# Down projection: half-width correction products in ten of eleven blocks, a merged first sum, and the scaling of e moved to the gate projection

## The reference, cut to what matters

```python
gu = _rmsnorm(h, g_ffn) @ w_gate_up                                  # FFN
h = h + (jax.nn.silu(gu[..., :D_FF]) * gu[..., D_FF:]) @ w_down      # down projection, D_FF = 5632
e = _rmsnorm(p_l @ w_ple, g_ple)
h = h + jax.nn.sigmoid(h @ w_ple_gate) * e                           # gate projection
return h                                                             # then a final _rmsnorm
```

## Time and profile before

| | |
|---|---|
| median of 3 runs | 1173.64 us (1172.48 to 1173.68) |
| span of the profiled execution | 1170.3 us |
| PE busy | 1159.2 us, 99% |
| DVE busy | 999.4 us, 85% |
| ACT busy | 562.8 us, 48% |
| chain that ended last | PE 94%, DVE 3%, DMA 1%, ACT 1%, issue 1% |
| granted clock of PE | 9 tenths or more of full speed (2.4 GHz) in all 40 slices |
| loads | 200 GB/s over the span, 65% of the DMA engines' time in the down stage |

### The profile page before, as it was taken

The page is one execution under the profiler, slowest core; times in us unless marked ns, Lnnn a source line. Parts: engine busy times, 40 slices in busy tenths (PEclk is TensorE's granted clock), DMA queues, the critical chain, the costliest instruction groups (busy, mean ns, idle before and its releaser), DMA issues.

```text
span 1170.3 us, 30909 instructions
## 1 busy us (share of the span) xinstructions
PE 1159.2 (99%) x12429; PEld 1039.3 (89%) x12429; DVE 999.4 (85%) x1563; ACT 562.8 (48%) x808; POOL 55.3 (5%) x80
## 2 busy tenths in 40 slices
PE   8999999999999999999999999999999999999997
PEld 7888988888888899899998999989989999999886
DVE  6788599678867898898989989888899999998687
ACT  6545654555545744443444444444444444444443
POOL 2122310100000200000000000000000000000000
PEclk9999999999999999999999999999999999999999
DMA  7767766766566566666666666666666666667561
GB/s 252 231 207 207 236 193 203 236 180 198 172 223 195 173 218 196 197 195 214 206 198 195 194 211 211 197 196 193 208 198 211 205 199 203 209 200 232 171 192 75
DMA packets 193386, 234.93 MB, mean 201 GB/s; under 512 B 8011, under 2 KB 153778, under 8 KB 193041
## 3 DMA queue, kind: packets, MB, share of 16 engines
q1 hardware_dynamic: 187984, 221.08, 60.2%
q0 software_dynamic: 3968, 11.89, 3.5%
q10 hardware_dynamic: 1360, 0.92, 0.3%
HBM read 226.89 MB, written 7.43 MB: 200 GB/s over the span
## 4 chain that ended last, share of the span: by engine, by line
PE 94%; DVE 3%; DMA 1%; ACT 1%; issue 1%; SPq 0%; DVEq 0%; ACTq 0%
PE acc L2293 13%; PE acc L1895 11%; PE acc L1897 11%; PE acc L1899 11%; PE acc L2334 7%; PE acc L2296 6%; PE acc L2295 6%; PE acc L2274 6%; PE acc L2276 5%; PE wrk L2274 4%; PE wrk L2276 4%; PE acc L2337 2%; PE acc L2336 2%; DMA raw<-in_w_in_dram 1%; DVE hl L970 1%; PE wrk L2052 1%
## 5 line engine op out<-in xcount | busy, mean ns | idle before, releaser
L970 DVE SCALAR_TENSOR_TENSOR hl<-raw,hl 128x1024 f16<-128x1024 f32 x414 | 492.9, 1218 | 58.7 <-ACT hl L606 56.0
L606 ACT ACTIVATE hl<-raw 128x1024 f16<-128x1024 f32 x414 | 420.5, 1052 | 172.3 <-DMA raw<-in_w_down_dram 90.4
L2293 PE MATMUL acc<-nrm,hl 128*128 128x264 f16 x1344 | 274.8, 276 | 0.0
L1897 PE MATMUL acc<-nrm,hl 128*128 128x264 f16 x920 | 253.9, 276 | 0.0
L1899 PE MATMUL acc<-nrm,hl 128*128 128x264 f16 x920 | 253.9, 276 | 0.0
L1895 PE MATMUL acc<-nrm,hl 128*128 128x264 f16 x920 | 253.9, 276 | 0.0
L2295 PE MATMUL acc<-nrm,hl 128*128 128x264 f16 x672 | 185.5, 276 | 0.0
L2296 PE MATMUL acc<-nrm,hl 128*128 128x264 f16 x672 | 185.5, 276 | 0.0
L2293 PEld LDWEIGHTS acc<-nrm,hl 128*128 128x128 f16 x1344 | 128.9, 98 | 17.8 <-DVE tg L1452 0.2
L2334 PE MATMUL acc<-big,hl 128*128 128x264 f16 x704 | 130.2, 276 | 0.0
L1895 PEld LDWEIGHTS acc<-nrm,hl 128*128 128x128 f16 x920 | 90.2, 98 | 13.1 <-issue 0.3
(11 more groups left out here) (493 smaller groups left out, 2226.3 us busy)
## 6 DMA issues: line engine op xcount, KB each, us to landing
raw<-in_w_gate_up_dram SPq DMA_DIRECT2D x168, 512.0 KB, 4.6
raw<-in_w_down_dram SPq DMA_DIRECT2D x88, 512.0 KB, 4.1
raw<-in_w_in_dram SPq DMA_DIRECT2D x80, 512.0 KB, 4.7
raw<-in_w_out_dram SPq DMA_DIRECT2D x32, 512.0 KB, 4.7
raw<-in_w_ple_gate_dram SPq DMA_DIRECT2D x32, 512.0 KB, 5.2
state<-in_state_hgrn_dram POOLq DMA_DIRECT2D x8, 512.0 KB, 7.2
out_new_hgrn_sample_dram<-state POOLq DMA_DIRECT2D x8, 512.0 KB, 5.2
raw<-in_w_gate_up_dram SPq DMA_DIRECT2D x16, 256.0 KB, 3.2
```

The lines of the kernel that those rows point to most:

```text
L606: nc.scalar.activation(hi[:, st.hl_slot(j, half), :], raw[:, st.raw_slot(j), :], ACT.Copy, scale=WSCALE).then_inc(hi_done, 1)
L970: stt(lo[:, st.hl_slot(j, half), :], raw[:, st.raw_slot(j), :], WSCALE, hi[:, st.hl_slot(j, half), :], ALU.mult, ALU.subtract).then_inc(lo ...
L1897: mm(out, wh, x_lo[:, kt, :], start=False, stop=False)
L2293: mm(out, wh, n_hi[:, kt, :], start=jj == 0 and kk == 0, stop=False, skip_group_check=bool(up))
```

## The change

The blocks of the down stage that use half-width corrections become 0 to 9, five pairs instead of four; only block 10 stays plain. The token sums cover 20 K-tile pairs instead of 16, in ten pieces instead of seven; new buffers and shared tiles (`s16_all`, `sf_all`, `pt_all`, `mixed`) hold them and what had lain there, and DVE waits once for the store out of `s_final`. In `hl` the high and low part of a slot now lie side by side, so that the sums of a pair read one regular pattern, and the first two sums are one operation of 2 x 8 x 128 elements, in which w12 is read twice through a step of 0. In DVE's down group the sums of pair 0 are made at the end of the group before, and the others move by one place. `scale_e` moves from the down groups into the gate groups, behind the fourth and fifth split of each, and in the last group behind split 5; `rstd_bc` moves to a tile of its own, and ACT no longer waits for `e_ready`.

```diff
-DOWN_PAIRS = (2, 4, 6, 8)
-DOWN_T = ((0, 8), (8, 10), (10, 12), (12, 13), (13, 14), (14, 15), (15, 16))
-T_SOON, T_LATE = (1, 3), (0, 2, 4, 5, 6)
+DOWN_PAIRS = (0, 2, 4, 6, 8)
+DOWN_T = ((0, 8), (8, 10), (10, 12), (12, 14), (14, 15), (15, 16), (16, 17), (17, 18), (18, 19), (19, 20))
+T_SOON, T_LATE = (1, 3, 6, 7, 8), (0, 2, 4, 5, 9)
...
-        hl = sb("hl", [P, 2, HL_SLOTS * BLOCK_KT * COLS], F16)
-        hi, lo = (hl[:, n, :].rearrange("p (s c) -> p s c", s=HL_SLOTS) for n in range(2))
+        hl = sb("hl", [P, HL_SLOTS, 2, BLOCK_KT * COLS], F16)
+        hi, lo = (hl[:, :, n, :] for n in range(2))
...
-            act.wait_ge(e_ready, KT)
...
             def weight_sums(s, s0, f, done, n):
 
-                w = hl[:, :, s0 * BLOCK_KT * COLS:(s0 + 2) * BLOCK_KT * COLS]\
-                    .rearrange("p h (q k m c) -> p h q k m c", k=2, m=2, c=P)
+                w = hl[:, s0:s0 + 2].rearrange("p s h c -> p (s h c)").rearrange("p (n k m c) -> p n k m c", k=2, m=2, c=P)
                 if f == 0:
-                    for k, x in enumerate((w[:, :, :, 1, 1], w[:, :, :, 0, 0])):
-                        last = tt(s[:, k], w[:, :, :, 0, 1], x, ALU.subtract)
-                    last.then_inc(done, 1)
+                    x, y = w[:, :, 0, 0], w[:, :, 0, 1].unsqueeze(1).to_broadcast([P, 2, 8, P])
+                    x = bass.AP(x.tensor, x.offset, [list(x.ap[0]), [3 * P, 2]] + [list(d) for d in x.ap[1:]])
+                    tt(s[:, 0:2], y, x, ALU.subtract).then_inc(done, 1)
                     return
                 dve.wait_ge(done, n + f)
-                x = w[:, :, :, 0, 0] if f == 1 else w[:, :, :, 1, 0]
-                tt(s[:, f + 1], x, s[:, 0 if f == 1 else 2], ALU.subtract).then_inc(done, 1)
+                tt(s[:, f + 1], w[:, :, f - 1, 0], s[:, f], ALU.subtract).then_inc(done, 1)
...
-                    dve.wait_ge(used, S_DOWN.block(i, j - 3 - (S_DOWN.bpg - 8 if u < 2 else 0)) + 1)
-                weight_sums(s_sum[u % 2], S_DOWN.hl_slot(j, half), f, down_sums, (i - 1) * DOWN_SUMS + 3 * u)
+                    dve.wait_ge(used, S_DOWN.block(i, j - 3 - (S_DOWN.bpg - 2 * len(DOWN_PAIRS) if u < 2 else 0)) + 1)
+                weight_sums(s_sum[(u + half) % 2], S_DOWN.hl_slot(j, half), f, down_sums, (i - 1) * DOWN_SUMS + 3 * u)
...
+            dve.wait_ge(sf_out, 16 * QUADS)
...
-                scale_e(0)
+                for f in range(3):
+                    down_sum(1, 1, 0, f)
                 for j in range(2, AHEAD):
                     split(S_DOWN, 1, j, 1)
...
-                sums(0)
                 split(S_DOWN, i, 4, half)
+                sums(1)
                 if evac:
                     evac()
                 else:
                     down_evac(i - 1, 1 - half)
                 split(S_DOWN, i, 5, half)
-                sums(1)
-                for j in range(6, 9):
-                    split(S_DOWN, i, j, half)
-                sums(2, (0,))
+                sums(2)
+                split(S_DOWN, i, 6, half)
+                split(S_DOWN, i, 7, half)
+                sums(3)
+                split(S_DOWN, i, 8, half)
                 next_low(i - 1)
                 split(S_DOWN, i, 9, half)
-                sums(2, (1, 2))
+                sums(4)
                 split(S_DOWN, i, 10, half)
-                sums(3)
                 ahead(0)
-                scale_e(i)
-                for j in range(1, AHEAD):
+                ahead(1)
+                if not nxt:
+                    for f in range(3):
+                        down_sum(i + 1, 1 - half, 0, f)
+                for j in range(2, AHEAD):
...
             def evac_gate(i):
+                dve.wait_ge(e_ready, i * TPG + TPG)
                 for n in range(TPG):
                     gate_tile(i, n)
...
-            group(S_GATE, 0, lambda: (dve.wait_ge(e_ready, KT), evac_gate(0)),
-                  between=lambda n: next_low(S_DOWN.groups - 1) if n == 1 else None)
+            def behind_split(i, n):
+
+                if n in (3, 4):
+                    scale_e(i * 2 + n - 3)
+
+            group(S_GATE, 0, lambda: evac_gate(0),
+                  between=lambda n: next_low(S_DOWN.groups - 1) if n == 1 else behind_split(0, n))
             with dve.Fori(1, S_GATE.groups - 1) as i:
-                group(S_GATE, i, lambda: evac_gate(i), between=lambda n: gained(i - 1) if n == 5 else None)
+                group(S_GATE, i, lambda: evac_gate(i), between=lambda n: gained(i - 1) if n == 5 else behind_split(i, n))
             last_gate = S_GATE.groups - 1
...
             split(S_GATE, last_gate, 5)
+            scale_e(2 * last_gate)
+            scale_e(2 * last_gate + 1)
             y_taken(0)
+            dve.wait_ge(e_ready, KT)
             gate_tile(last_gate, 0)
...
-                    u = j // 2 - DOWN_PAIRS[0] // 2
+                    u = (j - DOWN_PAIRS[0]) // 2
                     q = 2 * (j - DOWN_PAIRS[0])
-                    last = corrections(b, slot, s_sum[u % 2], 2 * (j % 2), ff_hi, ff_lo, 4 * j,
+                    last = corrections(b, slot, s_sum[(u + half) % 2], 2 * ((j - DOWN_PAIRS[0]) % 2), ff_hi, ff_lo, 4 * j,
```

More of the change, by code:

```diff
@@ L343, in build @@
         ps8 = sb("ps8", [P, 8])
-        lbt = sb("lbt", [P, 4, 8])
-        nomlb = sb("nomlb", [P, 8])
+        mixed = sb("mixed", [P, TOK])
+        at = [0, 64, 128, 192, 208, 224, 256, 264]
+        o_smp, o_sq, o_ms, ss_o, rs_o, lbt, nomlb = (mixed[:, a:b] for a, b in zip(at, at[1:]))
+        o_smp, o_sq, o_ms = (x.rearrange("p (h b) -> p h b", b=NSAMP) for x in (o_smp, o_sq, o_ms))
+        ss_o, rs_o = (x.rearrange("p (h a) -> p h a", a=2) for x in (ss_o, rs_o))
+        lbt = lbt.rearrange("p (n k) -> p n k", k=8)
         ss = sb("ss", [P, 3])
@@ L348, in build @@
         rt = sb("rt", [P, HEADS * 2])
[L349 to L355, removed]
+        pt_all = sb("pt_all", [P, 4 * TOK], F16)
+        pt_hi, pt_lo = (pt_all[:, 2 * n * TOK:2 * (n + 1) * TOK].rearrange("p (k t) -> p k t", t=TOK) for n in range(2))
+        dt16 = [x.bitcast(F16) for x in (mix[:, :], big[:, 2 * FFW:2 * FFW + 4 * TOK], spare[:, 660:660 + 4 * TOK])]
+        dt16 += [s16_all[:]]
+        dt16 += [x.rearrange("p a t -> p (a t)").bitcast(F16) for x in (a32[:], tg32[:], gate_t[:, 2:4])]
+        dt16 += [sf_all[:].bitcast(F16), pt_all[:], gate_t[:, 0:2].rearrange("p a t -> p (a t)").bitcast(F16)]
+        dt16 = [x.rearrange("p (h f q t) -> p h f q t", h=2, f=4, t=HALF_T) for x in dt16]
         h_sq, h_ssq = a32[:, 0, :], a32[:, 1, :]
         k_pack = a32[:].rearrange("p a t -> p (a t)")[:, 0:4 * P].rearrange("p (h t) -> p h t", h=4)
-        rstd_bc, smp_sums = gate_t[:, TPG - 1, :], gate_t[:, 0, 0:P]
+        rstd_bc, smp_sums = mixed[:], gate_t[:, 0, 0:P]
         diag, diag_smp = tg32[:, 0, 0:SEQ], tg32[0:NSAMP, 1, 0:NSAMP]
@@ L817, in _ @@
                     act.wait_ge(mean_ready, 2)
[L818 removed]
+                    nc.scalar.activation(rs_o, rs_o, ACT.Sqrt).then_inc(rstd_ready, 1)
                 if b == SAMPLE_ROOT_AT:
                     act.wait_ge(mean_ready, 3)
[L821 removed]
+                    nc.scalar.activation(o_sq, o_sq, ACT.Sqrt).then_inc(rstd_ready, 1)
                 if b in O_MIX_AT:
@@ L2172, in sample_sums @@
                 pe.wait_ge(osq_ready, 1)
-                mm(out[:, 0:64], ones[:], o_sq[:].rearrange("p h b -> p (h b)"), start=True, stop=True).then_inc(job_done, 1)
+                mm(out[:, 0:64], ones[:], o_sq.rearrange("p h b -> p (h b)"), start=True, stop=True).then_inc(job_done, 1)
                 yield
```

42 lines of the change are left out of this document (20 added, 22 removed).

## The result

The changed kernel takes **1194.97 us** (median of 4, 1193.43 to 1195.73) against 1173.06 us of the kernel before on the same chip: ratio 1.0189, 95% interval 1.0177 to 1.0201, that is 21.9 us more where 10.4 were forecast. The spans of the two profiled executions, 1170.3 and 1193.9 us, are 23.6 us apart; that is what is accounted for here. In each execution of the changed kernel 1.8 to 1.9 us lie around the span. So the 3.3 us that stood ahead of the prediction between span and median are not all around the program: the profiled execution of the kernel before (1170.3 + 1.8) is as quick as the shortest of its four, that of the changed kernel is the longest of its four, and so the spans lie further apart than the medians.

A forecast was written before the change was run, and what follows sets the result against it. PE bounds the whole kernel, but DVE becomes the down stage's bound at 29.6 us a group: 9.7 us there plus 1.0 at the tail, +10.7 on 1173.64, about 1184 us; range 1175 to 1195.

The forecast's parts named there:

- PE's gain: Down stage: ten of eleven blocks fast instead of eight, 2.66 us in all; PE alone falls to 27.80 us a group.
- the fused sum: Down pairs: the first two sums become one operation of 2048 elements, 1.25 us, 0.06 less a pair.
- VectorE's work: Down group: 29.25 us of DVE work against 27.80 us of PE, so DVE becomes the bound of the stage.
- The load waits: Down groups: DVE's waits for loads, taken as 0.35 us a group, between no wait and today's 1.07 us.
- late loads: Down stage: loads landing after 4 us and more instead of 3.5 add about 1 us over six groups.
- The bounds: Down group: 28.95 us with no wait, 30.7 with the extra 0.3 us and waits grown by half; 29.6 taken.
- The first group: First fast down group: DVE late through more early token sums; about 28.4 us, +0.2.
- The gate stage's start: Start of the gate stage: ACT loses its wait for e, worth nothing as PE runs there.
- The tail: Last gate group: two more scalings, 1.24 us less 0.23, put the kernel's end back by 1.0 us.
- a starting lead: Range: with load waits, the reason for 4 us on each side, as one execution can't size them.
- A rival's condition: Down stage, DVE stays hidden: needs a group of at most 27.8 us or 8.5 us lead; 1172.0 us; chance 0.13.

The follow-up runs named there:

- the run with four pairs: Changed kernel with the fifth pair alone taken back and the sums in their old places; layout, fused sum and moved scaling stay: 1172.91 us, ratio 1.0007.
- the two together: Changed kernel without the fifth pair and with the last gate group's e scaled earlier: 1172.04 us, ratio 0.9997 to the kernel before.
- the run with GpSimd: Changed kernel with the low halves of h and the scalings of e moved to GpSimd in the down groups: 1201.81 us, ratio 1.0251.

## Why the prediction was right and wrong

*PE's gain, the fused sum, VectorE's work: right.* Fast blocks come 2.51 us apart where PE does not wait, the fused sum takes 1.224 us for 1.25, VectorE's own work is 29.26 us a group for 29.25. That this last agrees to 0.01 us is luck: five fused sums at 0.026 us less make 0.13 us, so other terms were as much too small. Which engine takes over and where PE feels it came as said: PE waits at the sums, 34 times by up to 0.5 us at the dependent ones (L1533).

*The load waits: the step that failed.* The prediction set 0.35 us a group, "since DVE itself is now late", and 1 us in all for late loads: 3.1 us over the stage. The run with half-size loads shows 10.9 us over the stage, 1.59 us in a steady group. The 7.8 us between the two are what the down stage took beyond the forecast (7.7). Being late gives nothing here: SP's waits are on VectorE's own splits, so when VectorE is late the loads are issued as much later. How long a split waits is set by VectorE's work between the split that frees a slot and the one that needs it, and by how many loads fly together.

The prediction counted that work (5.1 us in place of 5.7) for block 2 alone, which split 10 releases and which waited before; in the new order block 2 waits for nothing. It passed over block 1, which split 9 releases. Before, 6.8 us lay between the end of split 9,

```profile
944.39 1.22 DVE L970 SCALAR_TENSOR_TENSOR hl<-raw,hl 128x1024 f16<-128x1024 f32 x1
```

and the split of block 1 (952.39 in the earlier trace rows). In the new order VectorE is there at 961.99, 5.0 us after split 9 (957.02), while the load (4.4), ACT (1.1) and the hand-overs between them take 5.8. And block 4, the fifth split, was to wait no longer; it waits 0.53 us, not for the copy of p1 but for its load, the third of a burst.

The bounds held the measured group: the terms of the upper one, 28.95 + 0.3 + 1.5 x 1.07, make 30.86 us (the 30.7 there is a slip), and 30.85 were measured. The value taken between the bounds was the wrong one.

*The first group:* 1.0 us over its old length, where 0.2 were set. With half-size loads it takes 28.23 us, and 28.4 were forecast: the rest is load waits again.

*The gate stage's start: a step that was missing.* The prediction looked at the gate stage for the moved scaling only, and called ACT's lost wait "worth nothing as PE runs there". It did not ask what stands ahead of `last_evac` in VectorE's and ACT's lists once VectorE is the bound. Of the 11.0 us by which the median passed the forecast, 5.2 us are there.

*The tail: right, a little too large.* 1.0 us was forecast; 0.7 us came, by the run with four pairs, by the run with the scalings earlier, and by the two together. The prediction had PE stand for DVE there before the change already; the profile of the kernel before lists no such wait, and that of the changed kernel lists 0.84 us.

In sum, against a forecast of 10.7 us on the span: 7.7 more in the down stage, 5.2 at the gate stage's start, 0.2 ahead of the stage, 0.3 less at the tail, 23.5 of the 23.6 us seen. The median of the changed kernel lies 11.0 us above the forecast and 0.03 us inside the range. That it lies inside is luck: the range was set for load waits and a starting lead, and 5.2 us come from the gate stage's start, which it did not have.

*A rival's condition:* for DVE to stay hidden, the lead asked for was 6 x 1.4 us. Against PE's own 27.80 us a group it is 6 x 1.8 = 10.8 us; with the 3.6 us read there, the rival was still less likely.

## What to carry to other kernels

When an edit turns an engine into the bound, do not take its waits as gone because it is late. If the loads that it waits for are released by its own progress, the waits come along. Look at each load by itself, in the new order of the list: the time from its release to its landing, with the loads that fly beside it, less the work that the engine has in between. Then go to the end of the stage and ask what the late engine still has ahead of the work that lets the next stage begin. And weigh the prize first: here 0.38 us a group of TensorE was bought with 2.7 us of sums on an engine that had 1.07 us to spare.

## What the runs showed of the hardware

A load of 512 KB landed 3.5 us after its issue when alone, 4.4 us when another had been issued 1.75 us ahead, 6.2 us as the third within 1.2 us. PE's idle time of 3.4 us at the gate stage's start was followed by a granted clock of 0.50 in the changed kernel. In the run with the scaling in the down groups it stayed at 1.00 after 3.3 us at the same place, while in the run with GpSimd it fell to 0.51 after 3.2 us. Much the same wait cost 3.5 us in one execution and 5.2 us in another, so a gap of that length can't be priced from one execution.
